# Attention of the last two prompt tiles moved into the expert gathers, with the third mixing group after it

## The reference, cut to what matters

```python
q, k, v, z, xbc, dt_raw, gates = split(rms_norm(x) @ w_in)
# differential attention, 8 heads, key width 64, value width 128, chunk-causal mask (CHUNK = 64)
s = q·k * 64**-0.5 - slope_h * |q_pos - k_pos|          # for each of two maps j
a = softmax(where(k_pos//64 <= q_pos//64, s, -1e30))
o = (a[:, :, 0] - lam * a[:, :, 1]) @ v
o_a = (rms_norm(o, sub_g) * (1 - lam_init)) @ w_attn_o
o_s = mamba2_scan(z, xbc, dt) @ w_ssm_o
x += (sigmoid(g_a) * o_a + sigmoid(g_s) * o_s) @ w_out   # the mixing
# PEER: 8 heads x top 16 of 128 x 128 experts, for each row of x
idx, g = product_key_top_k(rms_norm(x) @ wq)
x += sum_k gelu(h·u[idx_k]) * g_k * v[idx_k]
x += sigmoid(rms_norm(x) @ w_pg) * (p @ w_pe)            # the finish
y = rms_norm(x)
```

## Time and profile before

| | |
|---|---|
| time, median of 3 runs | 4658.14 us (4653.52 to 4663.47) |
| the profiled execution | 4661.18 us, span 4659.6 us |
| PE, DVE, ACT, POOL busy | 79%, 60%, 36%, 31% of the span |
| mean granted clock of PE | 0.892 |
| HBM traffic | 1399 MB, of it 1107 MB gathered expert rows |
| attention loop | from 1213.8 to 1511 us |
| first group's mixing, first choice | 1515 to about 1690 us |
| gathers | about 1660 to 4610 us |

### The profile page before, as it was taken

The page is one execution under the profiler, slowest core; times in us unless marked ns, Lnnn a source line. Parts: engine busy times, 40 slices in busy tenths (PEclk is TensorE's granted clock), DMA queues, the critical chain, the costliest instruction groups (busy, mean ns, idle before and its releaser), DMA issues.

```text
span 4659.6 us, 52828 instructions
## 1 busy us (share of the span) xinstructions
PE 3703.6 (79%) x16970; PEld 2165.9 (46%) x16970; DVE 2813.4 (60%) x6237; ACT 1683.9 (36%) x4983; POOL 1466.9 (31%) x1389
## 2 busy tenths in 40 slices
PE   8999998999898888777877878557666766766758
PEld 7998777999666764343322334212212212212212
DVE  4443214777466258666567667667666666666774
ACT  2222112355466013223323333234434444444433
POOL 1000002333110014434433444344444444444442
PEclk9999999999889999988888999778887878888879
DMA  3223323655223669999999999999999999999996
GB/s 113 74 83 120 106 77 115 193 190 171 91 83 95 208 238 381 418 380 404 404 362 391 417 409 420 420 420 414 417 417 411 407 420 414 404 420 415 414 408 264
DMA packets 316092, 1398.98 MB, mean 300 GB/s; under 512 B 38448, under 2 KB 113216, under 8 KB 180672
## 3 DMA queue, kind: packets, MB, share of 16 engines
q0 software_dynamic: 167728, 1166.48, 61.8%
q1 hardware_dynamic: 148112, 229.38, 14.5%
HBM read 1314.59 MB, written 81.16 MB: 300 GB/s over the span
## 4 chain that ended last, share of the span: by engine, by line
DMA 30%; PE 21%; DVE 8%; issue 4%; POOL 4%; ACT 1%; ACTq 0%; DVEq 0%; POOLq 0%
DMA peer_uv<-in_peer_uv_dram,peer_idx 30%; PE peer_acc L2841 10%; PE peer_fo L2780 4%; POOL peer_uv L1951 3%; DVE peer_uv L2097 3%; PE peer_fo L2793 2%; PE peer_fo L2680 2%; PE peer_tb L2624 1%; ACT peer_scaled L2415 1%; DVE peer_hot L2061 0%; DVE peer_hot L2058 0%; DVE peer_sel L2064 0%; ACT peer_ge L2410 0%; PE peer_acc L2729 0%; DVE peer_topi L2029 0%
## 5 line engine op out<-in xcount | busy, mean ns | idle before, releaser
L2097 DVE CUSTOM_DVE_ANT_0 peer_uv<-peer_uv,peer_rep 128x1024 f32<-128x1024 f32 x1056 | 1282.1, 1224 | 927.3 <-DMA peer_uv<-in_peer_uv_dram,peer_idx 893.0
L2841 PE MATMUL peer_acc<-peer_uv,peer_scaled 128*64 128x512 f32 (+1 forms) x4224 | 1308.4, 740 | 670.4 <-ACT peer_scaled L2415 653.0
L1951 POOL DMA_INDIRECT peer_uv<-in_peer_uv_dram,peer_idx x1056 | 1200.0, 1136 | 1728.4 <-PE peer_acc L2841 1478.4
L2841 PEld LDWEIGHTS peer_acc<-peer_uv,peer_scaled 128*64 128x64 f32 (+1 forms) x4224 | 311.3, 158 | 1512.3 <-ACT peer_scaled L2415 935.5
L2410 ACT ACTIVATE peer_ge<-peer_pre 128x1 f32<-128x1 f32 x1056 | 213.4, 202 | 1663.6 <-DVE peer_pre L2097 1662.6
L2780 PE MATMUL peer_fo<-peer_space 128*128 128x256 f32 (+2 forms) x1152 | 405.1, 494 | 99.6 <-DVE peer_space L2151 40.4
L99 PE MATMUL proj_bank<-proj_hTh,proj_wplead 128*128 128x352 f32 x1232 | 432.0, 351 | 1.8 <-DVE proj_wprest L91 1.8
L2415 ACT ACTIVATE peer_scaled<-peer_eased,peer_ge 128x64 f32<-128x64 f32 (+1 forms) x1056 | 366.4, 347 | 122.0 <-ACT peer_ge L2410 2.4
L100 PE MATMUL proj_bank<-proj_hTr,proj_wplead 128*128 128x352 f32 x1232 | 401.8, 326 | 0.0
L101 PE MATMUL proj_bank<-proj_hTh,proj_wprest 128*128 128x352 f32 x1232 | 401.5, 326 | 0.0
L2408 ACT ACTIVATE peer_eased<-peer_fold,peer_gw 128x64 f32<-128x64 f32 (+1 forms) x1056 | 350.9, 332 | 1.1 <-DVE peer_gw L2079 1.1
(11 more groups left out here) (362 smaller groups left out, 4930.9 us busy)
## 6 DMA issues: line engine op xcount, KB each, us to landing
proj_wp<-in_w_in_dram POOLq DMA_DIRECT2D x13, 2048.0 KB, 9.9
peer_space<-in_w_ssm_o_dram SPq DMA_DIRECT2D x48, 512.0 KB, 7.8
proj_scan<-scratch_acum SPq DMA_DIRECT2D x36, 512.0 KB, 4.7
peer_uv<-in_peer_uv_dram,peer_idx POOLq DMA_INDIRECT x1056, 12.7
proj_wp<-in_w_in_dram POOLq DMA_DIRECT2D x14, 1024.0 KB, 9.0
peer_space<-in_w_attn_o_dram SPq DMA_DIRECT2D x24, 512.0 KB, 7.9
peer_space<-in_w_out_dram SPq DMA_DIRECT2D x24, 512.0 KB, 7.8
scratch_xtok<-proj_shared SPq DMA_DIRECT2D x20, 512.0 KB, 3.2
```

The costliest lines, as they stand in the source:

```text
L1951: pool.indirect_dma_start(uv[k][:], None, io["peer_uv"], bass.IndirectOffsetOnAxis(ap=idx[t % 2][:, col:col + 1], axis=0)).then_inc(uv_in[ ...
L2097: dve.tensor_tensor_reduce(uv[k][:, 0:D], uv[k][:, 0:D], rep[j][:], 1.0, 0.0, ALU.mult, ALU.add, pre[:, k:k + 1]).then_inc(u_done, 1)
L2841: x = pe.matmul(acc[group(t, slot % groups_of(t)), h:h + HALF], scaled[slot][:, 0:r], uv[slot][:, D + h:D + h + HALF], start=(it == 0 and ...
```

## The change

1. The attention loop runs over tiles 0 to 5 and the sample rows (`ORDER`), seven steps a head instead of nine. It still loads the whole of q, k and v and stores all key rows; of `scratch_att` it stores 6 tiles instead of 8.
2. The attention of tiles 6 and 7 becomes 16 steps in the gather stage (`DSTEPS`, 8 heads by 2 tiles), seven slots each (`DSLOTS`), from slot 162 (`D0`) to slot 285 (`D1`). A step has seven units: four "score" units (two maps by two halves of up to 512 keys, PE; DVE adds the bias and takes the maximum), two "wturn" units (PE transposes the weights, ACT copies them) and one "values" unit. SP loads k, q and v of each head again, two heads ahead, and stores 64 KB for each step. POOL and DVE build the distances once; DVE halves them after each head.
3. The third group's mixing comes after it: its first turns at slot 292, its parts from 310 to 469 with `STEP` 5 instead of 8. All its loads wait for slot `D1`, since they share the space.
4. `LATE` gives tile 5 a preparation six iterations later, and `due` spreads the choice of tiles 2 and 5 over the iterations that are left.
5. The finish starts at iteration 76 instead of 60, one tile every 7 iterations instead of 9; steps 0 to 7 instead of 0 to 10.

```diff
-GROUPS = ((0, 1), (2, 3, 4), (5, 6, 7, NPT))
+EARLY, DEFERRED = (0, 1, 2, 3, 4, 5), (6, 7)
@@ differential_attention
-    STEPS = 2 * NT
+    ORDER = EARLY + (SAMPLE,)
+    NTILES = len(ORDER)
+    STEPS = 2 * NTILES
@@ retrieve_and_finish
-    STEP, GAP, HEAD = (6, 5, 8), 6, 20
-    LATE = [4 if t == GROUPS[1][0] else 0 for t in range(NT)]
+    STEP, GAP, HEAD = (6, 5, 5), 6, 20
+    LATE = [{GROUPS[1][0]: 4, GROUPS[2][0]: 6}.get(t, 0) for t in range(NT)]
+    ND = len(DEFERRED)
+    DSTEPS, DSLOTS, DHEAD, DTAIL = H * ND, 7, 22, 4
...
+        if g == NG - 1:
+            time += DHEAD - GAP + PE_AHEAD
+            D0 = time
+            for s in range(DSTEPS + 2):
+                if s >= 2:
+                    units.append(("values", s - 2, 0, 0, time, 1))
+                if s < DSTEPS:
+                    units += [("score", s, n // 2, n % 2, time + 1 + n, 1) for n in range(4)]
+                if 1 <= s <= DSTEPS:
+                    units += [("wturn", s - 1, n, 0, time + 5 + n, 1) for n in range(2)]
+                time += DSLOTS
+            D1 = time - DSLOTS + DTAIL
...
-    FIN_BASE, FIN_EVERY, FIN_LATE = 60, 9, LAST - 1
+    FIN_BASE, FIN_EVERY, FIN_LATE = 76, 7, LAST - 1
@@ due
-            return FIRST[tile - 1] + 6 + LATE[tile] + n * 3 // SEGS
+            return FIRST[tile - 1] + 6 + LATE[tile] + n * (15 - LATE[tile]) // (PAIRS * SEGS - 1)
@@ SP
+                def load_deferred_head(h):
+                    b = h % 2
+                    if h < 2:
+                        sp.wait_ge(h2_stored, h2_stores(1))
+                    else:
+                        sp.wait_ge(unit_made, unit_at["values", ND * (h - 2) + ND - 1, 0, 0] + 1)
+                    cols = slice(h * P, (h + 1) * P)
+                    sp.dma_start(dk[b], dr["chan"][C_K + h * P:C_K + (h + 1) * P, 0:SEQ]).then_inc(d_in[b], 16)
+                    sp.dma_start(dq[b], dr["chan"][cols, DEFERRED[0] * P:SEQ]).then_inc(d_in[b], 16)
+                    sp.dma_start(dv[b], io["v_prompt_out"].rearrange("(t p) c -> p t c", p=P)[:, :, cols]).then_inc(d_in[b], 16)
@@ DVE
+                def score_out(n, s, j, half):
...
+                    dve.tensor_tensor_reduce(de[j][b][:, first:last], bank[n % 2][:, 0:last - first], ddist[:, off + first:off + last], 1.0, -3.0e38,
+                                             ALU.add, ALU.max, dtop[b][:, 2 * j + half:2 * j + half + 1]).then_inc(unit_out, 1)
...
+                        if s % ND == ND - 1:
+                            dve.tensor_scalar(ddist, ddist, 0.5, None, ALU.mult).then_inc(d_slope, 1)
...
+                def combine_deferred(s):
...
+                    dve.scalar_tensor_tensor(out=dw[b][:, 0:e], in0=de[1][b][:, 0:e], scalar=dratio[b][:, 0:1], in1=de[0][b][:, 0:e],
+                                             op0=ALU.mult, op1=ALU.add).then_inc(d_w, 1)
@@ ACT
+                def exps_deferred(s):
...
+                        act.activation(de[j][b][:, 0:e], de[j][b][:, 0:e], ACT.Exp, bias=dntop[b][:, j:j + 1], scale=AK ** -0.5,
+                                       accum_out=dtot[b][:, j:j + 1]).then_inc(d_exp, 1)
```

More of the change, by code:

```diff
@@ L1361, in weights_out @@
                 def weights_out(i, m):
-                    r = P if m % NT < SAMPLE else DEC
-                    for g, blocks in enumerate(groups(m % NT)):
+                    r = rows_of(tile_of(m))
+                    for g, blocks in enumerate(groups(tile_of(m))):
                         j = turn_of["w", m, g]
@@ L1534, in retrieve_and_finish @@
     for g in range(NG):
+        if g == NG - 1:
[10 more added lines that the diff above has]
+            D1 = time - DSLOTS + DTAIL
+            time += 1
+            for at in range(2 * SIZE[g]):
+                units.append(("turn", g, 0, at, time, 1))
+                time += 2
+            time += 2
         for s in range(3):
@@ L1557, in ends, with outs, acts, deferred_tile @@
         return u[4] + u[5]
+    BY_ACT = ("wturn", "values")
+    def outs(n):
+        return sum(u[0] not in BY_ACT for u in units[:n + 1])
+    def acts(n):
+        return sum(u[0] in BY_ACT for u in units[:n + 1])
+    def deferred_tile(s):
+        return DEFERRED[s % ND]
+    def deferred_width(s):
+        return (deferred_tile(s) + 1) * P
+    def exps_at(s):
+        return D0 + DSLOTS * s + 6
+    def combine_at(s):
+        return D0 + DSLOTS * s + 9
+    def load_time(n, before, g):
+        return max(before, D1) if g == NG - 1 else before
     def group_of(t):
@@ L1888, in mixing @@
                         g, p, i = row_of(q - 2)
-                        if ends("turn", g, p, 2 * i + 1) == time:
+                        if load_time(q, ends("turn", g, p, 2 * i + 1), row_of(q)[0]) == time:
                             load_row(q)
@@ L2197, in mixing, with deferred @@
+                def deferred(time):
+                    for part in range(3):
+                        if time == D0 - 2 + part:
+                            distances(part)
+                    for s in range(DSTEPS):
+                        if time == combine_at(s):
+                            combine_deferred(s)
                 def mixing(time):
+                    deferred(time)
                     for n, (kind, g, p, m, start, length) in enumerate(units):
-                        if kind == "turn" and start + 2 == time:
+                        if kind == "score" and start - PE_AHEAD + 1 == time:
+                            score_out(n, g, p, m)
+                        if kind == "turn" and start + (1 - PE_AHEAD if (g, p) == (NG - 1, 0) else 2) == time:
@@ L2504, in finish, with weights_turned_out, values_out, deferred @@
                         act.activation(ft[0:r, :], fss[t % 2][0:r, :], ACT.Sqrt).then_inc(fin_act, 1)
+                def exps_deferred(s):
+                    b, e = s % 2, deferred_width(s)
+                    act.wait_ge(d_top, 2 * (s + 1))
+                    for j in range(2):
+                        act.activation(de[j][b][:, 0:e], de[j][b][:, 0:e], ACT.Exp, bias=dntop[b][:, j:j + 1], scale=AK ** -0.5,
+                                       accum_out=dtot[b][:, j:j + 1]).then_inc(d_exp, 1)
+                def weights_turned_out(n, s, half):
+                    first, last = 4 * half, min(4 * half + 4, deferred_tile(s) + 1)
+                    act.wait_ge(unit_made, n + 1)
+                    act.activation(dwT[s % 2][:, first:last, :], blocks(bank[n % 2], P)[:, 0:last - first, :], ACT.Copy).then_inc(unit_act, 1)
+                def values_out(n, s):
+                    act.wait_ge(unit_made, n + 1)
+                    if s >= 2:
+                        act.wait_ge(d_stored[s % 2], 16 * (s // 2))
+                    act.activation(drow[s % 2], bank[n % 2][:, 0:P], ACT.Copy, scale=dinv[s % 2][:, 0:1]).then_inc(unit_act, 1)
+                def deferred(time):
+                    for s in range(DSTEPS):
+                        if time == exps_at(s):
+                            exps_deferred(s)
+                    for n, (kind, s, half, _, start, _) in enumerate(units):
+                        if kind == "wturn" and start - PE_AHEAD == time:
+                            weights_turned_out(n, s, half)
+                        elif kind == "values" and start - PE_AHEAD + 1 == time:
+                            values_out(n, s)
                 def prepare_piece(t, it):
```

197 lines of the change are left out of this document (150 added, 47 removed).

## The result

The changed kernel takes 4692.16 us (median of 6 runs, 4684.16 to 4701.57), the kernel before beside it 4658.29 (6 runs): ratio 1.0072, 95% interval 1.006 to 1.0085. It is 34 us slower; 4637 was predicted, with a range up to 4676.

The account below looks back on a forecast made before the run. Engines bound the kernel up to about 1750 us, the 1 MB gathers after. Terms -80 + 33 + 14 + 6 + 4 + 0 + 2 = -21 us gave 4640 from 4661.2, 4637 as median; 8-in-10 range 4598 to 4676.

Parts of the forecast that it names:

- the front: Attention loop: removing tiles 6 and 7 of each of 8 heads gives back 80 us.
- DMA 33: DMA queues in the gathers: the moved attention's loads and stores cost 33 us.
- handovers 14: Gathers: DVE at 93% has next to no room, costing 14 us, a good microsecond a step.
- late v 6: Gathers: v loads may come 5 to 8 us late for six heads; cost 0 to 20 us, taken as 6.
- D1 4: Slot D1: the third group's 3 MB, asked for only four slots before its first turn, cost 4 us.
- tile 5's choice and the finish: Kernel's finish: it ends one iteration later, its pieces and tile 5's choice closer together; 2 us, 0 to 10.
- the third group: Third group's mixing at five slots a part instead of eight: no cost, with -10 to +15 us.
- rival 2: Moved attention's steps stop the gathers, costing 58 us; 4675 in all, slower above 3.1 us a step; chance 0.15.
- It fits: PE in the gathers: 10.9 us a head adds 0.78 us a slot to 1.49, within 2.7 to 2.8.
- rival 3: Third group's mixing: PE at its limit when DVE hands banks back late; +21 us, 4658; chance 0.15 with like cases.
- its sign: Third group's windows: 34 or fewer gathers in 100 us would show rival 3.

Follow-up runs that it names:

- e3: The kernel before with its attention loop over tiles 0 to 5 and the sample rows only, attention of tiles 6 and 7 left out: 4584.31 us, ratio 0.9844.
- e4: The changed kernel with the moved attention of tiles 6 and 7 left out (`DSTEPS` 0) and its slots kept empty: 4588.53 us, ratio 0.985.
- e1: The changed kernel with `LATE` of tile 5 at 0 instead of 6, so its preparation and choice start where they did before: 4675.34 us, ratio 1.0044.
- e8: The changed kernel with `LATE` 0, ACT's copies first, rows first at D1, head 1's load later, k and q apart from v: 4651.95 us, ratio 0.999.
- e10: e9 with DVE emptying the mixing's banks three slots earlier in the second and third group: 4621.3 us, ratio 0.9914.
- e2: The changed kernel with ACT's copies ahead of its exponentials within a slot: 4680.19 us, ratio 1.0052.
- e5: The changed kernel with the moved attention's exponentials replaced by scaled copies, so without table loads there (output not the reference's): 4677.53 us, ratio 1.0043.
- e6: The changed kernel with each head's v read as 128 rows of 4 KB instead of 1024 pieces of 512 bytes (wrong values): 4663.16 us, ratio 1.0015.
- e13: e10 with eight slots to a step of the moved attention rather than seven, starting two slots later: 4638.75 us, ratio 0.9958.
- e9: e8 with the front also storing each head's v as 128 rows of 4 KB, from which the moved attention loads it: 4655.23 us, ratio 0.9991.
- e12: The kernel before with only the earlier emptying of the banks in its second and third group: 4630.65 us, ratio 0.9938.
- e7b: The changed kernel with eight slots to a step of the moved attention rather than seven, starting two slots later: 4682.36 us, ratio 1.0046.

## Why the prediction was wrong

By its own terms, against differences of medians:

| term | predicted | measured |
|---|---|---|
| the front | -80 | -72 (e3) |
| moved attention: DMA 33, handovers 14, late v 6, D1 4 | +57 | +104 (e4): by the traces about 49 of DMA busy time and 54 lost |
| tile 5's choice and the finish | +2 | +13 to 17 (e1, the choice alone) |
| the third group | 0 | -9 to -13 (what is left of e4 less e3, the finish in it; by their traces -3 at slot 560, so not clear of 0) |
| sum | -21 | +34 (the rows above give 36, from medians of several sets of runs) |

1. **The front** came nearly as worked out, 72 by the medians and 79.5 at the first dot. A round of two heads takes 55.2 us instead of 75.0, from transposes of one round to those of the next:

```profile
1268.94 1.09 PE L1428 MATMUL attn_tp<-ident,attn_kT 128*128 128x128 f32 x8
...
1324.15 1.09 PE L1428 MATMUL attn_tp<-ident,attn_kT 128*128 128x128 f32 x8
```

2. **The stalls are the step that failed: for DVE "I take 14, a good microsecond a step", with 6 for late loads.** For these 20 us the stretch lost 48, 3.0 us a step, about the 3.1 at which rival 2 decides for slower; with slot D1's hole it is 54 for 24. Rival 2 had 0.15, and at 4675 it too was 17 us short. The mistake was to ask which engine is full. I took DVE at 2.55 us a slot, "93%"; its trace shows 284.2/127 = 2.24, 68% of the time that passed. DVE was not the cause, it was the one that waited (104.6 us for scores). A step is a chain of seven handovers between in-order queues: scores from PE to DVE, biased scores to ACT, exponentials to DVE, combined weights to PE, transposed weights to ACT, their copies to PE, the product to ACT. Each has dots, gelus or sums ahead of it.

   Late loads and order were more than half: with both mended (e8) 23 of the 54 are left. Handovers alone are then some 23 to 33 us (e8 to e10), 1.5 to 2 a step, twice what I took. e2 (order in one queue, 9 to 12), e5 (one link shorter, 14) and e6 (loads) each took a part; that the length of the chain sets the rest is argued from these, not shown, and e13, where more room made it slower, does not fit it.

3. **"PE: the 10.9 us of a head ... It fits" was too cheap.** PE by line and form, from 2111 to 2530 us (busy, mean ns, idle before):

```profile
L3002 PE MATMUL peer_fo<-peer_space 64*128 64x512 f32 x96 | 57.5, 704 | 23.7 <-DMA peer_space<-out_dram 15.0 <-DVE peer_dtop L2327 7.7 <-ACT peer_x L2598 1.1
...
L3020 PE MATMUL peer_fo<-peer_space 128*128 128x128 f32 x240 | 41.6, 343 | 40.3 <-ACT peer_space L2682 40.2
...
L3011 PE MATMUL peer_fo<-ident,peer_space 128*128 128x128 f32 x120 | 20.2, 301 | 8.0 <-DVE peer_dtop L2327 8.0
...
L3002 PE MATMUL peer_fo<-peer_space 64*128 64x384 f32 x32 | 15.5, 568 | 0.0
```

134.8 us busy, 16.9 a head, and 72 us of waiting. The scores are 9.1 a head against 5.1 in the loop: there the eight records of a tile run as one block, here in runs of two and four between other work, at a granted clock of 0.84 on average instead of 1.00 (which of the two costs how much was not tested). It fits on average, but it lies in the chain.

4. **The DMA term** (33) was 49 of busy time up to slot 310. The packets of SP's queue were priced right, 33 more than in e4; the gathers' own, dearer by 16 us in all, were not in the sum. Small packets beside them are not the reason, or not the only one: the gathers' packets took 296 ns in the stretch of the changed kernel and 291 in e5 with 9,400 packets of 512 bytes beside them, but also 293 in e6 and 296 in e9 with 2,000, and 291 in the same slots of the kernel before with none. On what small pieces cost an engine itself, the trace gives 28 ns for 512 bytes against 173 for 4 KB, so 1024 of the one cost 1.3 times as much as 128 of the other.

5. **Late v: "so it may need 25 to 30 us and be late"** named the right place, with 20.2 us of landing in the median, and forgot two loads of the same queue: tile 2's h2 rows behind the first heads (15.4 us of PE) and the rows at D1 behind the weights (16.8). For 6 + 4 us of the sum, 44 us of PE's waits stand in the trace.

6. **Tile 5's choice** was costed by density, "2 us". It cost one wait of 25.1 us, since `due` put a result behind the slot that needs it. No average shows that; the order of ACT's and DVE's queues at slot 608 would have.

7. **The third group** at five slots lost 31 us to banks emptied late where it lost 22 at eight, so rival 3 was right in kind, with 9 of its 21 us, and its sign was seen; on balance the term is not a loss. Rows 3 showed the fault before the change, a share of 0.93 from 2300 to 2400 us, which I took for a dip that stays in number. In the kernel before it was worth 28 us (e12, where the share in the same slots is 1.01).

The chances leaned on "only the front's is large and sure". The term next to it was bounded by 0 and 40 for DVE alone, while the four together could be 100.

Open is what makes up the 33 us still lost in slots 162 to 289 of e10, and why one slot more per step helps e7b and hurts e13. In e10 PE's largest wait there is for ACT's scaled columns, 64.9 us in 32 waits, and DVE's is for scores, 62.8; a run that changes only ACT's share of the work in e10 was not made.

## What to carry over

Work put under a transfer-bound stage is not paid by the average load of any engine alone: here no engine was over 73% busy in slots 162 to 289, and 48 us were lost. Write the chain of handovers down for one step, with the queue position of every link, before asking which engine is full. Check for each moved load what stands ahead of it in its queue, and for each moved result whether it is computed ahead of the slot that reads it. A DMA share of 0.93 in the kernel before was a bank handed back two slots late: mending that gave 28 us by a few shifted numbers, without the change (e12). e10, with the change and all the mends, is 36 us faster than the kernel before, but only some 9 of these are the change's.

## What the runs showed of the chip

- A load of 1024 pieces of 512 bytes landed in 7.9 us (median of eight) in the attention loop. Under the gathers it took 5.7 to 48.4 us in the changed kernel (median 20.2) and 4.8 to 50.7 in e8 (median 9.4), longest each time for the first two, issued beside other loads. As 128 rows of 4 KB it took 4.5 to 23.4 (e6, median 13.7).
- The gathers' packets took 281 ns in the stretch with next to none beside them (e4) and 291 to 296 with the moved attention's or the mixing's beside them (changed kernel, e5, e6, e9, before), whether those were small or long.
- The Trainium skill, DMA: Bandwidth & Descriptors, section SWDGE vs HWDGE vs iDMA, says that an engine takes turns between its internal queues and changes only at packet boundaries. The trace agrees in so far as v mostly lands later beside the gathers than in the attention loop; the same load with 64 packets an engine took from 5.7 to 28.9 us for the last six heads of one kernel, and no run here separates the turns from the rest.
- The exponential started at 2192.09, when the table load of 2190.79 had run 1.28 us. The Trainium skill, ScalarE: Activation LUTs, section What ACT_TABLE_LOAD costs, adds a drain of 1.38 us; the trace again shows none.
